# Turned probabilities copied once and unrounded, values on two halves of TensorE's columns, in the main attention of a hybrid decoder layer

## The reference

```python
def fox_attend(q, q_cum, q_pos, k, v, k_cum, k_pos):
    s = jnp.einsum('bqhd,bkhd->bhqk', q, k).astype(jnp.float32) * SCALE
    s = s + (q_cum.transpose(0, 2, 1)[:, :, :, None] - k_cum.transpose(0, 2, 1)[:, :, None, :])
    p = masked_softmax(s, k_pos[None, :] <= q_pos[:, None])
    return jnp.einsum('bhqk,bkhd->bqhd', p.astype(v.dtype), v)
...
    p_s = masked_softmax(s_s, (ok & (dist_s >= 0))[:, :, None])
    o_s = jnp.einsum('bghqs,bgqsd->bqghd', p_s.astype(vg.dtype), vg)
...
    p_w = masked_softmax(s_w, mask_w)
    o_w = jnp.einsum('bghqk,bkgd->bqghd', p_w.astype(vw.dtype), vw)
```

## Time and profile before

| | us |
|---|---|
| median of three runs | 2153.32 (2152.46 to 2153.6) |
| the profiled execution: its own time | 2154.1 |
| its span | 2152.4 |
| PE busy | 1891.2 (88%) |
| DVE busy | 996.4 (46%) |
| ACT busy | 732.7 (34%) |
| POOL busy | 575.7 (27%) |
| L2259 DVE subtraction, 288 times | 147.6, mean 533 ns |
| L2200 ACT rounded copy, 288 times | 131.9, mean 473 ns |
| L2125 PE transposes, 816 times | 138.9, mean 276 ns |

### The profile page before, as it was taken

The page is one execution under the profiler, slowest core; times in us unless marked ns, Lnnn a source line. Parts: engine busy times, 40 slices in busy tenths (PEclk is TensorE's granted clock), DMA queues, the critical chain, the costliest instruction groups (busy, mean ns, idle before and its releaser), DMA issues. The chain is left out here.

```text
span 2152.4 us, 32230 instructions
## 1 busy us (share of the span) xinstructions
PE 1891.2 (88%) x11816; PEld 1661.7 (77%) x11816; DVE 996.4 (46%) x1897; ACT 732.7 (34%) x1456; POOL 575.7 (27%) x684
## 2 busy tenths in 40 slices
PE   3998899996867398999999699899999999989995
PEld 2887677996634387888888578799999999866674
DVE  2333421333332246777777564323323333356997
ACT  2323321212211016777777543212111111133352
POOL 4310212434353322222221120211212212143452
PEclk9899899998998559999999989999999999989998
DMA  5443542354985832222220042111111111064543
GB/s 141 90 109 142 207 131 95 130 206 144 300 239 194 157 69 74 60 60 65 60 60 11 22 162 86 46 50 39 49 48 39 56 42 39 30 216 142 181 142 130
DMA packets 169576, 229.27 MB, mean 107 GB/s; under 512 B 44684, under 2 KB 112709, under 8 KB 169319
## 3 DMA queue, kind: packets, MB, share of 16 engines
q1 hardware_dynamic: 141690, 146.09, 22.5%
q0 software_dynamic: 27760, 81.55, 13.5%
HBM read 192.62 MB, written 40.18 MB: 108 GB/s over the span
## 5 line engine op out<-in xcount | busy, mean ns | idle before, releaser
L2259 DVE TENSOR_TENSOR pa_probs_T_lo<-pa_t,pa_probs_T_hi 128x512 fp32r<-128x512 f32 (+3 forms) x288 | 147.6, 533 | 64.8 <-ACT pa_probs_T_hi L2200 64.0
L121 PE MATMUL gate_acc<-o_T_hi,w_gate_split_hi 128*128 128x352 f32 x528 | 171.5, 325 | 2.0 <-ACTq L2638 2.0
L121 PE MATMUL up_acc<-o_T_hi,w_up_split_hi 128*128 128x352 f32 x528 | 170.4, 323 | 0.7 <-DVEq L2681 0.7
L122 PE MATMUL gate_acc<-o_T_lo,w_gate_split_hi 128*128 128x352 f32 x528 | 170.2, 322 | 0.0
L123 PE MATMUL gate_acc<-o_T_hi,w_gate_split_lo 128*128 128x352 f32 x528 | 170.0, 322 | 0.0
L122 PE MATMUL up_acc<-o_T_lo,w_up_split_hi 128*128 128x352 f32 x528 | 169.2, 320 | 0.0
L123 PE MATMUL up_acc<-o_T_hi,w_up_split_lo 128*128 128x352 f32 x528 | 169.1, 320 | 0.0
L2200 ACT ACTIVATE pa_probs_T_hi<-pa_t 128x512 fp32r<-128x512 f32 (+3 forms) x288 | 131.9, 473 | 90.8 <-PE pa_t L2125 87.5
L2125 PE MATMUL pa_t<-ident,pa_scores 128*128 128x128 f32 x816 | 138.9, 276 | 17.8 <-DVE pa_probs_T_lo L2259 17.8
L2185 ACT ACTIVATE pa_scores<-pa_scores,pa_neg_max 128x128 f32<-128x128 f32 (+1 forms) x192 | 143.3, 746 | 30.8 <-DVE pa_neg_max L2223 26.7
L121 PE MATMUL y_acc<-w_down_split_hi,act_split_hi 128*128 128x512 f32 x308 | 125.5, 407 | 19.8 <-DVE act_split_lo L3003 19.2
(11 more groups left out here) (442 smaller groups left out, 4770.7 us busy)
## 6 DMA issues: line engine op xcount, KB each, us to landing
w_down_raw<-in_w_down SPq DMA_DIRECT2D x59, 512.0 KB, 4.6
fox_k_pages<-in_cache_fox_kv SPq DMA_DIRECT2D x64, 256.0 KB, 7.0
w_rows<-in_cache_fox_kv POOLq DMA_DIRECT2D x64, 256.0 KB, 7.5
w_gate<-in_w_gu SPq DMA_DIRECT2D x22, 512.0 KB, 3.8
w_up<-in_w_gu SPq DMA_DIRECT2D x22, 512.0 KB, 3.8
w_rows<-in_w_in SPq DMA_DIRECT2D x5, 2048.0 KB, 10.2
sel_pages<-in_cache_nsa_kv POOLq DMA_DIRECT2D x64, 128.0 KB, 7.6
pa_k_fox<-scratch_kf_d POOLq DMA_DIRECT2D x32, 256.0 KB, 6.2
```

What stands on the lines that cost most here:

```text
L121: pe.matmul(out, a[0][at], b[0][bt], start=start, stop=False)
L122: pe.matmul(out, a[0][at], b[1][bt], start=False, stop=False)
L2259: dve.tensor_tensor(lo, PT[n % 2][:, 0:m * P].rearrange("p (m n) -> p m n", n=P), hi, ALU.subtract).then_inc(s_cd, 1)
```

## The change

The turned probabilities are copied out of PSUM once, as float32 and not rounded: even chunks by ACT, odd chunks by DVE. The values are float32 and not split; their DMA writes straight into the place from which PE reads. A key slot takes one matmul call, with float32 operands and 64 stationary columns. Slots alternate between two halves of PE's columns (output partitions 0 to 63 and 64 to 127), and `back` adds the two halves as before. PE's pieces of values are now whole pairs of slots. PE waits for two copy counters (`s_ca`, `s_cd`) and for the value loads themselves; the counter of finished values goes up twice per pair.

```diff
-        self.v = {kind: [ph.sb(f"pa_v_{kind}{u}", [P, NT, 2, HD], FR) for u in range(2)] for kind in kinds}
-        self.v_raw = [ph.sb(f"pa_v_raw{u}", [P, NT, HD]) for u in range(2)]
+        self.v = {kind: [ph.sb(f"pa_v_{kind}{u}", [P, NT, HD]) for u in range(2)] for kind in kinds}
...
-    def split_values(self, pool, dst, raw, sem, at):
-
-        pool.tensor_copy(dst[:, 0:NT, 0, :], raw[:, :, :]).then_inc(self.s_vh, 1)
-        pool.wait_ge(self.s_vh, at)
-        pool.tensor_tensor(dst[:, 0:NT, 1, :], raw[:, :, :], dst[:, 0:NT, 0, :], ALU.subtract).then_inc(sem, 1)
...
-                if n >= 2:
-                    sp.wait_ge(pa.s_gs, n - 1)
...
-                sp.dma_start(g_raw[n % 2][:, :, :], src.rearrange("(t p) e -> p t e", p=P)).then_inc(pa.s_gv[n], 16)
+                sp.dma_start(pa.v[kind][u][:, :, :], src.rearrange("(t p) e -> p t e", p=P)).then_inc(pa.s_gv[n], 16)
...
-        pT = [split(ph, f"pa_probs_T{i}", [P, NT + 1, 2, P]) for i in range(2)]
+        pT = [ph.sb(f"pa_probs_T{i}", [P, NT + 1, 2, P]) for i in range(2)]
...
+        def done(p):
+
+            return 2 * max(0, p + 1) + 1
...
-            for both in pT:
-                for t in both:
-                    for slot, half in ((0, 0), (NT, 1)):
-                        pool.tensor_copy(t[:, slot, half, :], c.zero[:, :].to_broadcast([P, P])).then_inc(s_z, 1)
+            for t in pT:
+                for slot, half in ((0, 0), (NT, 1)):
+                    pool.tensor_copy(t[:, slot, half, :], c.zero[:, :].to_broadcast([P, P])).then_inc(s_z, 1)
...
                 if n >= 2:
-                    pe.wait_ge(s_cd, n - 1)
+                    pe.wait_ge((s_ca, s_cd)[n % 2], n // 2)
...
-                n = 2 * len(mine)
-                begin, end = math.ceil(n * begin), math.ceil(n * end)
+                n = len(mine)
+                begin, end = (2 * math.ceil(n / 2 * part) for part in (begin, end))
                 if begin == 0 and end > 0:
-                    pe.wait_ge(s_cd, of_unit[2 * p + 1][-1] + 1)
+                    last = of_unit[2 * p + 1][-1]
+                    pe.wait_ge(s_ca, last // 2 + 1)
+                    pe.wait_ge(s_cd, (last + 1) // 2)
                     if t == 0 and kind == "fox":
-                        pe.wait_ge(pa.s_vs[u], i + 1)
-                    if t == 0 and kind == "sel":
-                        pe.wait_ge(pa.s_gs, 4)
+                        pe.wait_ge(pa.s_fv[u], 16 * i + 16)
+                    if t == 0 and kind != "fox":
+                        pe.wait_ge(pa.s_gv[2 * u + (kind == "win")], 16)
                     pe.wait_ge(s_n, max(1, p))
-                for y in range(begin, end):
-                    slot, key = mine[y // 2]
-                    ins = pe.matmul(O[p % 2][:, 0:2 * P], v[kind][u][:, key, :, :].rearrange("p w e -> p (w e)"),
-                                    pT[p % 2][y % 2][:, slot, :, :].rearrange("p a n -> p (a n)"),
-                                    start=y == 0, stop=y == n - 1)
-                    if y == n - 1:
+                for y in range(begin, min(end, n)):
+                    slot, key = mine[y]
+                    side = y % 2 * HD
+                    ins = pe.matmul(O[p % 2][side:side + HD, 0:2 * P], v[kind][u][:, key, :],
+                                    pT[p % 2][:, slot, :, :].rearrange("p a n -> p (a n)"), start=y < 2, stop=y >= n - 2)
+                    if y >= n - 2:
                         ins.then_inc(s_o, 1)
...
-                    for n in of_unit[e]:
-                        _, a, m = chunks[n]
-                        slot = slots(e)[a][1]
-                        act.wait_ge(s_t, n + 2)
-                        act.activation(pT[p % 2][0][:, slot:slot + m, e % 2, :], PT[n % 2][:, 0:m * P].rearrange("p (m n) -> p m n", n=P),
-                                       ACT.Copy).then_inc(s_ca, 1)
+                    for n in of_unit[e]:
+                        if n % 2 == 0:
+                            _, a, m = chunks[n]
+                            slot = slots(e)[a][1]
+                            act.wait_ge(s_t, n + 2)
+                            act.activation(pT[p % 2][:, slot:slot + m, e % 2, :], PT[0][:, 0:m * P].rearrange("p (m n) -> p m n", n=P),
+                                           ACT.Copy).then_inc(s_ca, 1)
...
+                    dve.wait_ge(s_o, done(e // 2 - 2))
                     for n in of_unit[e]:
-                        _, a, m = chunks[n]
-                        slot = slots(e)[a][1]
-                        hi, lo = (pT[e // 2 % 2][w_][:, slot:slot + m, e % 2, :] for w_ in range(2))
-                        dve.wait_ge(s_ca, n + 1)
-                        dve.tensor_tensor(lo, PT[n % 2][:, 0:m * P].rearrange("p (m n) -> p m n", n=P), hi, ALU.subtract).then_inc(s_cd, 1)
+                        if n % 2 == 1:
+                            _, a, m = chunks[n]
+                            slot = slots(e)[a][1]
+                            dve.wait_ge(s_t, n + 2)
+                            dve.tensor_copy(pT[e // 2 % 2][:, slot:slot + m, e % 2, :],
+                                            PT[1][:, 0:m * P].rearrange("p (m n) -> p m n", n=P)).then_inc(s_cd, 1)
```

More of the change, by code:

```diff
@@ L1730, in __init__ @@
         self.s_gv = [ph.sem(f"pa_group_v_loaded{n}") for n in range(4)]
-        self.s_vh = ph.sem("pa_v_rounded")
-        self.s_vs = [ph.sem(f"pa_fox_v_split{u}") for u in range(2)]
-        self.s_gs = ph.sem("pa_group_v_split")
     def load_fox(self, pool, d, h, u):
@@ L1745, in load_fox_values @@
     def load_fox_values(self, sp, d, h, u):
-        sp.dma_start(self.v_raw[u][:, :, :], d["fox_kv_p"][0, 0, :, 1, ds(h, 1), :].rearrange("(t p) a e -> p t (a e)", p=P)).then_inc(self.s_fv[u], 16)
-    def split_values(self, pool, dst, raw, sem, at):
-        pool.tensor_copy(dst[:, 0:NT, 0, :], raw[:, :, :]).then_inc(self.s_vh, 1)
-        pool.wait_ge(self.s_vh, at)
-        pool.tensor_tensor(dst[:, 0:NT, 1, :], raw[:, :, :], dst[:, 0:NT, 0, :], ALU.subtract).then_inc(sem, 1)
+        sp.dma_start(self.v["fox"][u][:, :, :], d["fox_kv_p"][0, 0, :, 1, ds(h, 1), :].rearrange("(t p) a e -> p t (a e)", p=P)).then_inc(self.s_fv[u], 16)
 def compressed_attention(c, pa):
@@ L1761, in compressed_attention @@
         pT = [ph.sb(f"ca_probs_T{i}", [NC, H, P]) for i in range(2)]
-        g_raw = [ph.sb(f"pa_group_v_raw{n}", [P, NT, HD]) for n in range(2)]
         mx = ph.sb("ca_max", [P, 2, H])
@@ L1791, in _ @@
                             pool.dma_start(pa.k[kind][u][w_][r * HD:(r + 1) * HD, :], d[src][w_, u]).then_inc(pa.s_kl[u], 16)
[L1792 to L1797, removed]
         U = 4
@@ L2005, in prompt_attention @@
         block = ph.block()
+        def done(p):
+            return 2 * max(0, p + 1) + 1
         def fox_free(eng, i, u):
-            eng.wait_ge(s_o, i * (NJ * PJ) + (3 * u + 1) * PJ + 1)
+            eng.wait_ge(s_o, i * (2 * NJ * PJ) + 2 * (3 * u + 1) * PJ + 1)
             settled(eng, c)
         def nsa_free(eng, i, u):
-            eng.wait_ge(s_o, i * (NJ * PJ) + (3 * u + 3) * PJ + 1)
+            eng.wait_ge(s_o, i * (2 * NJ * PJ) + 2 * (3 * u + 3) * PJ + 1)
             settled(eng, c)
@@ L2070, in turn @@
                         pa.load_fox(pool, d, h + 1, u)
-                    if kind == "sel":
-                        pool.wait_ge(pa.s_fv[u], 16 * i + 32)
-                        settled(pool, c)
-                        pa.split_values(pool, v["fox"][u], pa.v_raw[u], pa.s_vs[u], 2 * i + u + 7)
                     if kind == "win":
@@ L2088, in _ @@
             pe.sem_inc(s_bk, 1)
-            pe.wait_ge(s_z, 12)
+            pe.wait_ge(s_z, 8)
             def scores(s):
@@ L2188, in _ @@
                     p = (s - 6) // 2
-                    act.wait_ge(s_o, p + 2)
+                    act.wait_ge(s_o, done(p))
                     act.wait_ge(s_bk, max(0, p - 1) + 1)
@@ L2194, in _ @@
                     p = e // 2
[L2195 removed]
+                    act.wait_ge(s_o, done(p - 2))
                     for n in of_unit[e]:
[L2197 to L2201 removed]
+                        if n % 2 == 0:
[4 more added lines that the diff above has]
+                                           ACT.Copy).then_inc(s_ca, 1)
         @block.vector
```

1 line of the change is left out of this document (removed).

## The result

The changed kernel takes 2166.1 us (median of 7, 2162.1 to 2167.7) against 2155.4 us for the kernel before (7 runs beside it): a ratio of 1.0045, 95% interval 1.0031 to 1.0058. It is slower by some 10 us, 0.45%. The forecast was 2156 us, +2.7 us on a kernel before of 2153.3. Measured is +10.7, so the change came out 8 us larger than forecast; the other 2 us are the kernel before, whose median of seven runs is 2155.4. The time lies above the forecast's own 2149 to 2163 and inside 2138 to 2182, in the case that the text called "stands come back" and gave a chance of 0.14.

A forecast was written before the change was run, and what follows sets the result against it. PE was taken to lead, with some 55 us idle: work 100 + 60 - 110 = +50 us, after idle time +4.4, then - 0.95 - 0.3 = +3.1 on 2154.1, forecast 2156 us; own range 2149 to 2163, wider 2138 to 2182.

The forecast's parts named there:

- stands come back: Rival: one more PE stand of 0.3 to 0.4 us in each of 24 jobs, +9 us, 2166; chance 0.14.
- What bounds the kernel: Changed stage: PE leads, busy 379 of 414 us, but idle some 55 us in 24 jobs behind the copy chain.
- The values, 100 us for 464 calls: PE's value matmuls: 232 pairs of calls at 0.431 us, both halves running at once, 100 us against 110 before.
- The rival of 2 x 50 us more: PE's value matmuls: the two halves of columns don't overlap, +100 us, 2256; chance 0.03.
- The rival of uncovered weight loads: PE's value pairs: a half's weights don't load under matmuls, +49 us, 2205, or 2180 if one stays uncovered; chance 0.10.
- The switches, 60 us: PE's 191 value pieces: 0.14 us each to get in, 0.15 out to transposes or 0.20 to scores.
- Tiles 4 and 5: Sel job: one piece adds 0.30 us, with no idle time there to pay for it.
- What the idle time pays: PE's waits in the jobs: sel +2.1 - 1.7 = +0.4 us, fox +0.15, win 0.0; eight rounds +4.4 us.
- Tiles 0 and 1 of sel and win: Sel job: three pieces add 0.80 us; all 0.93 of idle goes but 0.1 at the output copy.
- Tiles 2 and 3 of sel and win: Sel job: +0.51 us of work; idle 0.97 becomes 0.46, a stand of 0.6 staying before the values.
- Tiles 6 and 7 of win: Win job: the stand before the values, longer than in sel, goes, taking 0.74 us of idle; whole job 0.0.
- The small parts: Zeroing copies on POOL -0.95 us, tail's subtraction -0.3; POOL's splits and PE's new load waits worth nothing.

The follow-up runs named there:

- e8: Changed kernel with the long chain of before: ACT copies every chunk, then DVE copies it again to the same place; 2201.0 us, ratio 1.0209.
- e7: Kernel before with the short chain alone: each chunk copied once, by ACT or DVE in turn, rest part left out; 2110.7 us, ratio 0.9788.
- e4: Changed kernel with the half of PE's columns changing after every second key slot, pairs of only two slots alternating as before; 2221.6 us (one run).
- e9: Changed kernel with DVE's output copy ahead of its chunk copies on odd steps, the job's coefficients left behind them; 2155.2 us, ratio 1.0002.
- e1: Changed kernel with DVE's output copy and the job's coefficients ahead of its chunk copies on odd steps; 2159.9 us, ratio 1.0024.
- e2: Kernel before with DVE's output copy and the job's coefficients ahead of its subtractions on odd steps; 2139.4 us, ratio 0.9926.

## Why the prediction was right or wrong

**What bounds the kernel.** Right. Each part of the change, tried alone, moved the time by about PE's work (e8) and about PE's idle time (e7). The forecast is the small difference of these two: +50 of work less 46 of idle time. The second was 9 us too large, twice the difference itself. That the error fell on the side of the forecast's sign, and did not turn it, is luck.

**The values, 100 us for 464 calls.** Right. Two slots cost 0.43 (1.01 - 0.58), forecast 0.431. The rival of 2 x 50 us more is ruled out by e4, in which that is what happened to the pieces of two slots. The rival of uncovered weight loads (from 0.22 for a pair of starts) did not happen: 2 x 0.2155 holds within the pieces. The Trainium skill, TensorE: Matmul & The Clock Gate, Part 3 (The mechanism), says in its list of what overlaps that a weight load overlaps matmuls in flight only when the row group differs; the 0.43 for two slots on the same rows contradicts it, and the measurement decides.

**The switches, 60 us.** Right to some hundredths where it can be read: last transposition of 875.74 + 3 x 0.109 = 876.07 to the values at 876.28 is 0.21 (0.109 + 0.09 forecast), and a piece of two slots holds PE for 0.58 (0.05 + 0.431 + 0.09 forecast, plus 0.01). Tiles 4 and 5, the place without any idle time to pay with, grew by 0.33 in 24 jobs, forecast 0.30. The Trainium skill, TensorEngine Tiling (Array Packing), Key Properties, says that changing the tiling mode drains TensorE; the trace agrees, with the 0.09 each way that it gave before.

**What the idle time pays.** This is the step that failed. The prediction let 1.7 to 2.1 us per job come back, 5.75 us for three jobs, 46 us in all; with PE's +6.3 and the measured +1.67 for three jobs, 4.6 us came back, 37 in all. The mechanism was right (the chain is shorter and the stands shrink); the size of what stays was not. By place:

- Tiles 0 and 1 of sel and win: forecast -0.03, measured +0.12. I left 0.1 for the stand at the output copy; the row at 873.37 shows 0.20.
- Tiles 2 and 3 of sel and win: forecast 0.0 (0.51 of work against 0.51 of idle), measured +0.14 and +0.11. The chain was right, its start wrong. I let DVE's copy begin 0.1 us after the last transposition by PE's spacing of 0.109; it begins 0.1 after the end of that transposition's record, 0.27 long: 876.86 + 0.65 = 877.51, and DVE starts at 877.62. (The 80 of these copies before which DVE was idle start 0.106 after it by the median.) The values start at 878.66, a stand of 0.73 behind the last transposition (877.82 + 0.109) where 0.6 was forecast; the 0.13 is what the pair of tiles grew by, to a hundredth.
- Tiles 6 and 7 of win: forecast -0.24, measured +0.01. Here the stand of 0.74 was to go; the values are still 0.69 behind their transposes, and where nothing waits it is 0.54 (875.74 to 876.28). Three operations of DVE stand ahead of them:

```profile
903.46 0.82 DVE L2206 CUSTOM_DVE_ANT_0 pa_scores<-pa_s,pa_bias_win 128x640 f32<-128x640 f32 x1 [1.08 <-PE pa_s L2089]
...
904.21 0.69 DVE L2243 COPY pa_probs_T<-pa_t 128x512 f32<-128x512 f32 x1
904.81 0.28 DVE L2216 COPY pa_job_out<-pa_o 128x128 f32<-128x128 f32 x1
```

  DVE waits for the scores, then does bias and maximum, and the copies follow it. Putting the output copy ahead (e9) takes only 0.05 off (4.47). So this place is not the order of the two copies; that it is the bias ahead of both is read from the rows and was not tried.
- Tiles 6 and 7 of sel: forecast +0.15, measured +0.20.
- Fox: forecast +0.15 for the job, measured +0.32.

The stands of tiles 0 to 3 end at DVE's output copy behind a turned copy. e1 and e9 show it by taking that order away: each of these pairs in sel and win loses 0.24 to 0.25, and with e9 10 of the 13.9 us of the stage go, which leaves +3.7 where the forecast for it was +4.4. The rival "the stands come back elsewhere" priced the right size (2166) and put it elsewhere, at ACT's order or DVE's bias before its copies. Most of the stands did not come back, they had not left; only tiles 6 and 7 of win, some 0.25 us in 8 jobs or 2 us, look like that rival. The chances held that case at 0.14, too low for a wait that the profile of before showed 30 times.

**The small parts.** Right in the main. PE's first wait for POOL fell by 0.9, forecast 0.95. No wait of PE for a load stands in the list after. The tail, from the last pair's first scores to the end of the stage, is 0.9 us shorter (427.0 - 414.2 against 414.0 - 400.3), forecast 0.3. DVE fell to 224 us where the prediction said 210; half of the 147.6 us of subtractions taken from 298 is 224. That the splits on POOL ahead of the stage are worth nothing can't be read: the kernels with the splits begin the stage at 802.1 to 811.9, those without at 801.7 to 807.5, and the two overlap.

**Left open.** The halves cost 55 us with the short chain and 45 to 48 with the long one, against 50 of work. The wait for the output copy is 3.7 us in e7 and 12.5 in the kernel after, which is the size of the excess with the short chain; no run puts the output copy first in e7, so this is read from the lists and not shown. Whether the rounding of pieces to whole pairs of slots has a share was not tried apart.

## What to carry to other kernels

Ask of each stand which instruction ends it and what stands ahead of that one in its own engine's queue: here PE waited 30 times for a small copy that needed nothing but its turn, and moving that copy ahead (e2, 2139.4 us) is worth more than what the whole change moved the time by. The change relieved DVE and ACT, which did not bound, and lengthened PE, which did. Price both parts of a change with two effects apart: this one is some -46 and +45 us. Compare under the same order on both sides: with the output copy first in both kernels the change costs 14 us and not 10. And after a change that makes it dear to switch between kinds of work, look at the order again: one piece instead of several gains 0.4 to 0.9% in the changed kernel and costs 1.5% in the old one.

## What the runs showed of the hardware that was not expected

- Work on two halves of PE's columns overlaps without strict alternation: two slots on one half and then two on the other took the same 1.08 to 1.09 us as alternating ones, but a piece of two slots all on one half took 1.01 instead of 0.58, although the next slots of the same pair were on the other half (e4).
- DVE and ACT, where they wait for transposes, start about 0.1 us after the end of the last one's record and not after its slot in PE's stream: 877.51 to 877.62 on DVE, while PE's transposes are 0.109 apart and 0.27 long. Over the stage of the kernel after the median is 0.106 for 80 copies of DVE and 0.096 for 95 of ACT.
- float32 values on half of the columns cost PE about as much as the split ones on all (100 against 110 us); it is the 191 pieces, at 0.3 us each by the prediction's prices, that make the change dear.
